# When GpSimd adds the squares of a new residual: after the input splits instead of among them

## The chip, the cores and the metric

The kernel runs on one core of one Trainium2 chip. The metric is the device time of one execution in microseconds (us), the median of several runs. A core has five engines that matter here: TensorE (PE in the profile; its weight loads are PEld), VectorE (DVE), ScalarE (ACT), GpSimd (POOL) and the DMA queue of SyncE (SP). They run side by side, each through its own list of instructions, and wait for each other on semaphores.

## The reference

Two stacks of two layers, one after the other, over 256 tokens (272 with 16 meta tokens in the first stack) with 1024 features, all in float32. In the second stack each branch ends in

```
h = h + weight * rms_norm(y, post_gain)       # y: output of an FFN, of the recurrent block or of attention
x = rms_norm(h, pre_gain)                     # input of the next branch
rms_norm(v, g) = v * rsqrt(mean(v * v) + 1e-6) * g
swiglu(x) = (silu(x @ w_gate) * (x @ w_up)) @ w_down
```

The branches of the second stack are, in order: FFN, recurrent block, FFN, keys and values with the next FFN, attention, FFN. Between two of them `h` gets a new value, and the next branch needs that value in two forms: as the input of its matrix products, and as the mean of its squares over the 1024 features.

## The kernel before, in words

The tensors lie transposed in SBUF: 128 features on the partitions, 8 slices of 128 features (k = 0 to 7), tokens along the free dimension. Each product of float32 tensors is made of three matmuls of split values: ScalarE rounds a tensor to its high part (`xhi`, `whi`), VectorE subtracts to get the low part (`xlo`, `wlo`), and TensorE adds up wlo x xhi, whi x xlo and whi x xhi. A tile of output (128 features) of an input of 8 slices is 24 matmuls. Weights stream through a ring of four slots: DMA to `raw`, ScalarE makes `whi` (line 885), VectorE makes `wlo` (line 1263).

The norm of the input is not put into the input. The matmuls run on `h` times its gain, and the factor 1/rms (`rstd`) is multiplied in when VectorE reads a tile out of PSUM. So the matmuls of a branch can begin before the sum of squares is there; the sum is only needed before the first tile is read.

The stages around the change are the six *updates*, numbered u = 7 to 12. Update 7 follows the first stack (VectorE scales `h` by the final norm, line 1768). Updates 8 to 12 add a branch output to `h` in VectorE's `update` (lines 1553 to 1587). For the slices 2 to 7 it works in pairs: scale a pair of `y` by `rstd` (line 1557), make the low parts of the pair before (line 1274), wait for its own pipeline, add into `h` (line 1562). After the low part of slice 7 it makes `wlo` of ring slot 3 of the next branch. These five updates have the same list of instructions. Meanwhile

- ScalarE (`inputs_from_h`, lines 1091 to 1104) makes the high parts of each pair (line 913) and then the squares of the pair (line 1104). The four pairs of squares go to `sil`, `z[0:2]`, `z[2:4]` and again `z[0:2]`; for the fourth it waits on `h_added` until GpSimd has read the second;
- GpSimd (`of_update`, lines 1807 to 1816) adds each pair of squares to `sil` as soon as ScalarE has made it (three adds of 128 x 512, line 1812), then adds the two halves of `sil` into `acc` (128 x 256, line 1816) and signals `sq_made`;
- TensorE runs `first_tiles` (lines 556 to 581): three tiles at once, 72 matmuls in the order of the slices, waiting before each slice for its low part (`x_lo_made`). Slices 6 and 7 come last, for tile 0, then 1, then 2. Then tile 3 (24 matmuls, lines 521 to 523), then `norm_sum` (line 532), which waits for `sq_made` and multiplies `acc` by a matrix of 1/1024. Behind it in TensorE's order stand tiles 4 to 7, which have PSUM banks of their own, and all later ones. `norm_sum` feeds ScalarE's square root (line 889), VectorE's reciprocal (line 1268), and by that the first reads of tiles.

ScalarE makes the next `whi` of slots 0, 1 and 2 when tiles 0, 1 and 2 are done; VectorE makes their `wlo` right after each; then comes the reciprocal, then slot 3. The order on every engine is the order of the program's lines; nothing is planned at run time.

In the listing, line numbers are those of the profile.

Of the kernel before, what the change touches and what calls it, by code (L numbers as in the profile page):

```python
# [19 lines left out]
T = SEQ + N_META  # L20
# [20 lines left out]
ALU = mybir.AluOpType  # L41
# [182 lines left out]
def program(nc, a):  # L224
    with ExitStack() as ctx:
# [4 lines left out]
        def at(name, shape, dt, where=None):  # L230

            place = top if where is None else where
            size = int(np.prod(shape[1:])) * (1 if dt == U8 else 4)
            h = nc.alloc_sbuf_tensor_at(name, shape, dt, offset=place[0])
            place[0] += (size + 31) // 32 * 32
            assert place[0] <= end, (name, place[0] - end)
            return h
# [11 lines left out]
        z = at("z", [P, 4, T], F32)  # L249
        sil = at("sil", [P, 2, T], F32)  # L250
        sqt = at("sqt", [P, 2, T], F32)
# [101 lines left out]
        def sem(name):  # L353
            return ctx.enter_context(nc.semaphore(name))
# [7 lines left out]
        h_made, x_hi_made, x_lo_made = sem("h_made"), sem("x_hi_made"), sem("x_lo_made")  # L362
        sq_made, sum_made, std_made, rstd_made = sem("sq_made"), sem("sum_made"), sem("std_made"), sem("rstd_made")

        y_sq, sq_added, h_sq, h_added = sem("y_sq"), sem("sq_added"), sem("h_sq"), sem("h_added")
        silu_made = sem("silu_made")
        hid_made, hid_hi_made, hid_lo_made = sem("hid_made"), sem("hid_hi_made"), sem("hid_lo_made")

# [40 lines left out]
        def layer_stage(l, which):  # L409
            q, j, n = ((0, 0, 0), (FFN_QUADS, FFN_TILES, 1), (FFN_QUADS + MIX_QUADS, FFN_TILES + MIX_TILES, 4))[which]  # L410
            return dict(q=l * LAYER_QUADS + q, j=l * LAYER_TILES + j, x=l * 3 + which, n=l * 5 + n,
                        f=l * 2 + which // 2, c=0)
# [466 lines left out]
        def _(act):  # L879
# [30 lines left out]
            def x_hi(x, k, c, to=xhi):  # L910

                at_k = bass.ds(k, 1) if not isinstance(k, int) else slice(k, k + 1)
                act.activation(to[:, at_k, c:T], h[:, at_k, c:T], ACT.Identity, scale=gain(x, k)).then_inc(x_hi_made, 1)  # L913
# [66 lines left out]
            def mixer(l):  # L980
                st = layer_stage(l, 1)
                q, j, x, n = st["q"], st["j"], st["x"], st["n"]
                for step, i in MIXER:
# [36 lines left out]
                    elif step == "turn_v":  # L1020
                        for s, (_, size) in enumerate(TOKEN_TILES):
                            act.wait_ge(v_turned, l * 3 + s + 1)
                            act.activation(vtok[0:size, s, :], bank[4 + s][0:size, :], ACT.Copy).then_inc(v_taken, 1)
# [23 lines left out]
                    elif step == "turn_v2":  # L1047
                        for s, (_, size) in enumerate(TOKEN_TILES):
                            act.wait_ge(v2_turned, l * 3 + s + 1)
                            act.activation(vtok2[0:size, s, :], bank[4 + s][0:size, :], ACT.Copy).then_inc(v2_taken, 1)  # L1050
# [40 lines left out]
            def inputs_from_h(x, u, c, to=xhi):  # L1091

                for s in range(4):
                    if s == 0:
                        act.wait_ge(h_made, 5 * (u - 7) + 1)
                        x_hi(x, 0, c, to)
                    act.wait_ge(h_made, 5 * (u - 7) + s + 2)
                    if s > 0:
                        x_hi(x, 2 * s, c, to)
                    x_hi(x, 2 * s + 1, c, to)  # L1100
                    if s == 3:
                        act.wait_ge(h_added, 3 * (u - 7) + 1)
                    squared = (sil[:, :, c:T], z[:, 0:2, c:T], z[:, 2:4, c:T], z[:, 0:2, c:T])[s]
                    act.activation(squared, h[:, 2 * s:2 * s + 2, c:T], ACT.Square).then_inc(h_sq, 1)

            def recurrent():
# [43 lines left out]
                for m in range(KD):  # L1150
# [3 lines left out]
                    if m == 7:  # L1154
                        norm_std(n + 1, c)
                    split_hi(q + 6 + m // RING, m % RING, CH8, j + 32 + m + 1)
                inputs_from_h(9, 9, c)

            def conv_hi(m):
# [21 lines left out]
            def attention():  # L1181
# [25 lines left out]
                for m in range(KD):  # L1207
                    act.wait_ge(tile_done, j + 8 + m + 1)
                    branch_out(n + 1, m, bank[4 + m % 2], j + 8 + m + 1, vcol("mix_post", 8 + m))
                    if m == 7:  # L1210
                        norm_std(n + 1, c)
                    split_hi(q + 3 + m // RING, m % RING, CH8, j + 8 + m + 1)
                inputs_from_h(13, 12, c)

            act.wait_ge(brow_done, 1)
# [18 lines left out]
            with act.Fori(0, DEPTH) as l:  # L1234
# [4 lines left out]
                ffn_down(**layer_stage(l, 2))  # L1239
            norm_std(10, 0)  # L1240
            inputs_from_h(7, 7, N_META)
            ffn(**F4)
            ffn_down(**F4, post=12)
# [551 lines left out]
        def _(pool):  # L1795
# [8 lines left out]
                        op = pool.tensor_tensor(acc[:, c:T], acc[:, c:T], sqt[:, k % 2, c:T], ALU.add)  # L1804
                op.then_inc(sq_made, 1)

            def of_update(u, last_sum):

                c = N_META
                for s in range(1, 4):  # L1810
                    pool.wait_ge(h_sq, 4 * (u - 7) + s + 1)
                    pool.tensor_tensor(sil[:, :, c:T], sil[:, :, c:T], z[:, 2 * ((s - 1) % 2):2 * ((s - 1) % 2) + 2, c:T],
                                       ALU.add).then_inc(h_added, 1)
                    pool.drain()
                pool.wait_ge(sum_made, last_sum)
                pool.tensor_tensor(acc[:, c:T], sil[:, 0, c:T], sil[:, 1, c:T], ALU.add).then_inc(sq_made, 1)

            def of_branch(n):

                c, done = N_META, branch_tiles(n) - 8  # L1820
                for m in range(1, 7):
                    pool.wait_ge(y_sq, done + m + 1)
                    pool.tensor_tensor(acc[:, c:T], acc[:, c:T], sqt[:, m % 2, c:T], ALU.add).then_inc(sq_added, 1)
                    if m < 6:
                        pool.drain()
                pool.drain().then_inc(sq_made, 1)

            def ffn(q, j, x, n, f, c, main_norm=True):
                with pool.Fori(0, KF // 2) as b:
                    for p in range(2):  # L1830
                        i = b * 2 + p
                        pool.wait_ge(silu_made, f * KF + i + 1)
                        pool.wait_ge(tile_read, b * RING + j + 2 * p + 2)
                        pool.tensor_tensor(z[:, 2 + p, c:T], sil[:, p, c:T], z[:, 2 + p, c:T],  # L1834
                                           ALU.mult).then_inc(hid_made, 1)
                        pool.wait_ge(hid_hi_made, f * KF + i + 1)
                        at_i = bass.ds(i, 1)
                        pool.tensor_tensor(hidlo[:, at_i, c:T], z[:, 2 + p:3 + p, c:T],  # L1838
                                           hidhi[:, at_i, c:T].bitcast(F32), ALU.subtract).then_inc(hid_lo_made, 1)
# [35 lines left out]
            def of_layer(st):  # L1875
                squares_of(h, 0, st["n"] + 1, lambda k: pool.wait_ge(tile_read, st["j"] + 2 * KF + k + 1))
# [9 lines left out]
            with pool.Fori(0, DEPTH) as l:  # L1886
# [2 lines left out]
                mixer(l)  # L1889
                ffn(**layer_stage(l, 2))  # L1890
                of_layer(layer_stage(l, 2))
            of_update(7, 11)
            ffn(**F4)
            of_branch(12)
            of_update(8, 13)
            for m in range(KD):
                pool.wait_ge(cv_hi_made, m + 1)
                pool.tensor_tensor(cvlo[:, m, :], cv[:, m, :], cvhi[:, m, :].bitcast(F32),
# [14 lines left out]
                    out_low(m - 1)  # L1913
            out_low(KD - 1)
            of_branch(14)
            of_update(9, 15)
            ffn(**F5)
            of_branch(16)
            of_update(10, 17)
            ffn(**F6)  # L1920
            of_branch(18)
            of_update(11, 19)
            of_branch(20)
            of_update(12, 21)
            ffn(**F7)
            of_branch(22)

# [81 lines left out]
```

## Time and profile before

| | |
|---|---|
| median of 3 runs | 2534.74 us (2528.47, 2534.74, 2535.23) |
| profiled execution | 2533.5 us, its span 2531.5 us |
| mean granted TensorE clock | 0.958 of full speed |
| TensorE busy | 93% of the span |
| VectorE, ScalarE, GpSimd busy | 59%, 47%, 24% |
| DMA | 150 GB/s over the span |

The span runs from the first instruction to the last of the profiled execution; every time of a row is counted from its start. An engine's busy time counts its instructions alone, not its waits. TensorE's clock has two levels, full (1.00 in the profile's column, 2.4 GHz) and half (0.50, 1.2 GHz). The end of a matmul is modelled, so for TensorE the distance from start to start is more telling than the time of one.

### The profile page before, as it was taken

The page shows a single profiled execution, that of the slowest core. Times are in us where ns is not written, and L with a number is a line of the kernel's source. Part 1 is how long each engine was busy: PE and PEld are TensorE (multiplying, and loading weights), DVE is VectorE, ACT ScalarE, POOL GpSimd, SP SyncE. Part 2 cuts the span into 40 slices and gives each one's busy share as a digit, 9 for nine tenths or more (in the row PEclk, how much of TensorE's full clock was granted, in tenths as well). Part 3 has the DMA queues.
Part 4 walks back from the last instruction along what each step waited for, and adds up shares of the span by engine and source line. Part 5 has one row for each costly group of instructions (what it writes and reads, how often), then busy time and mean ns, then how long its engine had stood idle before and what let it go on. Part 6 is the DMA issues. An engine that isn't in the chain of part 4 may idle for free.

```text
span 2531.5 us, 49922 instructions
## 1 busy us (share of the span) xinstructions
PE 2351.9 (93%) x18064; PEld 2266.5 (90%) x18064; DVE 1502.3 (59%) x1960; ACT 1191.4 (47%) x1739; POOL 604.3 (24%) x617
## 2 busy tenths in 40 slices
PE   7999988899999999879999989986899999977998
PEld 7999876699999999875899989986899899977998
DVE  6556775465555557873655565477654755465653
ACT  5445542344444436432354355456654545445552
POOL 4221130043213210310232233123331122111320
PEclk9999997899999999987999999998999999998999
DMA  6554332245545544321355445533455465531653
GB/s 209 174 183 156 115 116 66 67 160 182 178 158 174 191 145 147 100 92 42 109 178 182 164 148 190 193 118 116 151 192 198 147 202 184 197 117 63 200 195 108
DMA packets 99267, 380.27 MB, mean 150 GB/s; under 512 B 10911, under 2 KB 13087, under 8 KB 99144
## 3 DMA queue, kind: packets, MB, share of 16 engines
q1 hardware_dynamic: 99144, 378.63, 45.6%
q8 instruction: 77, 1.26, 0.2%
q14 instruction: 46, 0.38, 0.1%
HBM read 377.52 MB, written 3.16 MB: 150 GB/s over the span
## 4 chain that ended last, share of the span: by engine, by line
PE 63%; issue 25%; DVE 5%; POOL 4%; ACT 1%; POOLq 1%; DVEq 1%; DMA 0%; ACTq 0%; SPq 0%
PE bank L523 20%; PE bank L521 20%; PE bank L522 20%; POOL kd L1863 2%; DVE h L1562 1%; PE bank L564 1%; DVE xlo L1274 1%; PE bank L566 1%; PE bank L565 1%; POOL midlo L1871 1%; DVE rstd L1268 0%; DVE wlo L1263 0%; DVE y L1557 0%; POOLq L1802 0%; ACT whi L885 0%
## 5 line engine op out<-in xcount | busy, mean ns | idle before, releaser
L1263 DVE TENSOR_TENSOR wlo<-raw,whi 128x1024 fp32r<-128x1024 f32 (+1 forms) x660 | 886.5, 1353 | 525.3 <-ACT whi L885 523.6
L521 PE MATMUL bank<-xhi,wlo 128*128 128x272 f32 (+1 forms) x3392 | 981.6, 289 | 3.2 <-DVE wlo L1263 2.0
L523 PE MATMUL bank<-xhi,whi 128*128 128x272 f32 (+1 forms) x3392 | 976.3, 288 | 0.0
L522 PE MATMUL bank<-xlo,whi 128*128 128x272 f32 (+1 forms) x3392 | 974.3, 287 | 0.0
L885 ACT ACTIVATE whi<-raw 128x1024 fp32r<-128x1024 f32 (+1 forms) x660 | 728.8, 1117 | 452.9 <-PE bank L523 429.5
L521 PEld LDWEIGHTS bank<-xhi,wlo 128*128 128x128 f32 x3392 | 647.4, 191 | 5.0 <-DVE wlo L1263 2.3
L523 PEld LDWEIGHTS bank<-xhi,whi 128*128 128x128 f32 x3392 | 646.8, 191 | 0.0
L522 PEld LDWEIGHTS bank<-xlo,whi 128*128 128x128 f32 x3392 | 646.1, 190 | 0.4
L523 PE MATMUL bank<-hidhi,whi 128*128 128x272 f32 (+1 forms) x1408 | 400.1, 284 | 0.0
L521 PE MATMUL bank<-hidhi,wlo 128*128 128x272 f32 (+1 forms) x1408 | 399.9, 284 | 0.0
L522 PE MATMUL bank<-hidlo,whi 128*128 128x272 f32 (+1 forms) x1408 | 399.1, 283 | 0.0
L1834 POOL TENSOR_TENSOR z<-sil,z 128x272 f32<-128x272 f32 (+1 forms) x176 | 164.5, 935 | 600.9 <-DVE z L1300 471.8
L522 PEld LDWEIGHTS bank<-hidlo,whi 128*128 128x128 f32 x1408 | 265.5, 189 | 0.0
L523 PEld LDWEIGHTS bank<-hidhi,whi 128*128 128x128 f32 x1408 | 264.8, 188 | 0.0
L521 PEld LDWEIGHTS bank<-hidhi,wlo 128*128 128x128 f32 x1408 | 264.7, 188 | 0.0
L1838 POOL TENSOR_TENSOR hidlo<-z,hidhi 128x272 f32 (+1 forms) x176 | 167.1, 949 | 131.0 <-ACT hidhi L939 131.0
L913 ACT ACTIVATE xhi<-h,vec 128x256 fp32r<-128x256 f32 (+2 forms) x104 | 50.8, 512 | 245.0 <-DVE h L1318 176.4
L939 ACT ACTIVATE hidhi<-z 128x272 f32 (+3 forms) x176 | 74.8, 425 | 133.3 <-POOL z L1834 133.3
L1293 DVE TENSOR_TENSOR z<-bank,rstd 128x272 f32<-128x272 f32 (+1 forms) x176 | 75.8, 430 | 80.3 <-PE bank L523 79.9
L564 PE MATMUL bank<-xhi,wlo 128*128 128x256 f32 (+1 forms) x240 | 76.6, 319 | 42.3 <-DVE xlo L1274 30.5
L1300 DVE TENSOR_TENSOR z<-bank,rstd 128x272 f32<-128x272 f32 (+1 forms) x176 | 75.7, 430 | 63.2 <-PE bank L523 63.2
L1274 DVE SCALAR_TENSOR_TENSOR xlo<-h,vec,xhi 128x256 fp32r<-128x256 f32 (+2 forms) x104 | 63.9, 629 | 54.2 <-ACT xhi L913 54.2
(307 smaller groups left out, 2760.1 us busy)
## 6 DMA issues: line engine op xcount, KB each, us to landing
raw<-ffn_gu SPq DMA_DIRECT2D x352, 512.0 KB, 3.5
raw<-ffn_down SPq DMA_DIRECT2D x128, 704.0 KB, 4.1
raw<-mix SPq DMA_DIRECT2D x120, 512.0 KB, 3.5
raw<-rec SPq DMA_DIRECT2D x28, 512.0 KB, 4.0
raw<-kv SPq DMA_DIRECT2D x16, 512.0 KB, 4.2
raw<-att SPq DMA_DIRECT2D x16, 512.0 KB, 4.2
bias_rows<-rows SPq DMA_DIRECT2D x8, 256.0 KB, 4.3
bias<-bias_rows SPq DMA_DIRECT2D x1, 1536.0 KB, 7.9
```

What stands on the lines that cost most here:

```text
L521: pe.matmul(out, wlo[:, slot, w], xh(i), start=(i == 0), stop=False)
L522: pe.matmul(out, whi[:, slot, w], xl(i), start=False, stop=False)
L523: mm = pe.matmul(out, whi[:, slot, w], xh(i), start=False, stop=(i == last))
L564: pe.matmul(out, wlo[:, k, w], hi[:, i, at_c:], start=(i == 0), stop=False)
L885: act.activation(whi[:, k, 0:cols], raw[:, k, 0:cols], ACT.Copy).then_inc(hi_made, 1)
L939: act.activation(hidhi[:, at_i, c:T], z[:, 2 + p:3 + p, c:T], ACT.Copy).then_inc(hid_hi_made, 1)
L1263: dve.tensor_tensor(wlo[:, k, 0:cols], raw[:, k, 0:cols], whi[:, k, 0:cols].bitcast(F32), ALU.subtract).then_inc(lo_made, 1)
L1274: dve.scalar_tensor_tensor(to[:, at_k, c:T], h[:, at_k, c:T], gain(x, k), hi[:, at_k, c:T].bitcast(F32), ALU.mult, ALU.subtract).then_inc( ...
L1293: dve.tensor_tensor(z[:, p, c:T], bank[banks[2 * p]][:, 0:T - c], rstd[:, c:T], ALU.mult).then_inc(tile_read, 1)
L1300: dve.tensor_tensor(z[:, 2 + p, c:T], bank[banks[2 * p + 1]][:, 0:T - c], rstd[:, c:T], ALU.mult).then_inc(tile_read, 1)
L1834: pool.tensor_tensor(z[:, 2 + p, c:T], sil[:, p, c:T], z[:, 2 + p, c:T], ALU.mult).then_inc(hid_made, 1)
L1838: pool.tensor_tensor(hidlo[:, at_i, c:T], z[:, 2 + p:3 + p, c:T], hidhi[:, at_i, c:T].bitcast(F32), ALU.subtract).then_inc(hid_lo_made, 1)
```

## The change

GpSimd's `of_update` now waits, before its first add, until all eight low parts of the next input are made (`x_lo_made`, 8 for each input x), and then makes the same four adds in the same order. The fourth pair of squares goes to a buffer of its own, `sqt`, instead of `z[0:2]`, so that ScalarE need not wait for an add, and the semaphore `h_added` goes. The calls get the number of the input that the update makes: 7, 8, 9, 10, 12, 13.

```
# ScalarE, inputs_from_h
-                    if s == 3:
-                        act.wait_ge(h_added, 3 * (u - 7) + 1)
-                    squared = (sil[:, :, c:T], z[:, 0:2, c:T], z[:, 2:4, c:T], z[:, 0:2, c:T])[s]
+                    squared = (sil[:, :, c:T], z[:, 0:2, c:T], z[:, 2:4, c:T], sqt[:, :, c:T])[s]
                     act.activation(squared, h[:, 2 * s:2 * s + 2, c:T], ACT.Square).then_inc(h_sq, 1)
# GpSimd
-            def of_update(u, last_sum):
+            def of_update(u, x, last_sum):
                 c = N_META
-                for s in range(1, 4):
-                    pool.wait_ge(h_sq, 4 * (u - 7) + s + 1)
-                    pool.tensor_tensor(sil[:, :, c:T], sil[:, :, c:T], z[:, 2 * ((s - 1) % 2):2 * ((s - 1) % 2) + 2, c:T],
-                                       ALU.add).then_inc(h_added, 1)
+                pool.wait_ge(x_lo_made, 8 * x + 8)
+                for s, squared in enumerate((z[:, 0:2, c:T], z[:, 2:4, c:T], sqt[:, :, c:T])):
+                    pool.wait_ge(h_sq, 4 * (u - 7) + s + 2)
+                    pool.tensor_tensor(sil[:, :, c:T], sil[:, :, c:T], squared, ALU.add)
                     pool.drain()
                 pool.wait_ge(sum_made, last_sum)
                 pool.tensor_tensor(acc[:, c:T], sil[:, 0, c:T], sil[:, 1, c:T], ALU.add).then_inc(sq_made, 1)
# the calls
-            of_update(7, 11)
+            of_update(7, 7, 11)
...
-            of_update(12, 21)
+            of_update(12, 13, 21)
```

## Rows read from the trace of the kernel before

**Rows 1.** The page: busy time by engine, and the chain by engine.
```profile
PE 2351.9 (93%) x18064; PEld 2266.5 (90%) x18064; DVE 1502.3 (59%) x1960; ACT 1191.4 (47%) x1739; POOL 604.3 (24%) x617
...
PE 63%; issue 25%; DVE 5%; POOL 4%; ACT 1%; POOLq 1%; DVEq 1%; DMA 0%; ACTq 0%; SPq 0%
```

**Rows 2.** Timeline of VectorE in update 8: start, time, engine, line, operation, tiles, shapes.
```profile
1671.96 0.69 DVE L1562 SCALAR_TENSOR_TENSOR h<-y,h 128x512 f32<-128x512 f32 x1
...
1674.22 1.80 DVE L1562 SCALAR_TENSOR_TENSOR h<-y,h 128x512 f32<-128x512 f32 x1
...
1677.59 1.82 DVE L1562 SCALAR_TENSOR_TENSOR h<-y,h 128x512 f32<-128x512 f32 x1
1679.99 0.88 DVE L1274 SCALAR_TENSOR_TENSOR xlo<-h,vec,xhi 128x256 fp32r<-128x256 f32 x2 [0.58 <-ACT xhi L913]
1680.79 1.22 DVE L1263 TENSOR_TENSOR wlo<-raw,whi 128x1024 fp32r<-128x1024 f32 x1
```

**Rows 3.** Timeline of GpSimd in update 8; in brackets its idle time and releaser.
```profile
1674.19 1.28 POOL L1812 TENSOR_TENSOR sil<-sil,z 128x512 f32<-128x512 f32 x1 [15.59 <-ACT z L1104]
1677.57 1.29 POOL L1812 TENSOR_TENSOR sil<-sil,z 128x512 f32<-128x512 f32 x1 [2.09 <-ACT z L1104]
1680.95 2.22 POOL L1812 TENSOR_TENSOR sil<-sil,z 128x512 f32<-128x512 f32 x1 [2.09 <-ACT z L1104]
1683.33 1.52 POOL L1816 TENSOR_TENSOR acc<-sil 128x256 f32<-128x256 f32 x1 [0.16 <-issue]
1693.77 0.80 POOL L1898 TENSOR_TENSOR cvlo<-cv,cvhi 128x256 fp32r<-128x256 f32 x1 [8.92 <-ACT cvhi L1161]
```

**Rows 4.** Timeline of TensorE in update 8: start of tile 3, then the norm's sum.
```profile
1682.80 0.28 PE L521 MATMUL bank<-xhi,wlo 128*128 128x256 f32 x1
...
1685.63 0.59 PE L532 MATMUL bank<-acc,consts 128*128 128x256 f32 x2
```

**Rows 5.** Windows on TensorE, updates 7 to 12, first matmul to norm's sum: stretch, length, busy, clock.
```profile
1474.94:1488.79 13.85, 13.62 (x97) 0.85 0.04 7
1671.01:1685.63 14.62, 14.47 (x96) 0.79 0.13 40
1793.77:1808.41 14.64, 13.25 (x96) 0.90 0.14 40
1991.02:2005.64 14.62, 13.54 (x96) 0.88 0.13 40
2235.44:2250.07 14.63, 13.93 (x96) 0.83 0.13 41
2328.42:2343.03 14.61, 13.62 (x97) 0.86 0.14 41
```

**Rows 6.** Timeline of VectorE in short windows: first and second `wlo` after update 8.
```profile
1682.75 1.51 DVE L1263 TENSOR_TENSOR wlo<-raw,whi 128x1024 fp32r<-128x1024 f32 x1 [0.72 <-ACT whi L885]
...
1684.17 1.76 DVE L1263 TENSOR_TENSOR wlo<-raw,whi 128x1024 fp32r<-128x1024 f32 x1
```

**Rows 7.** Timeline of ScalarE after update 8: three `whi`.
```profile
1681.65 2.96 ACT L885 ACTIVATE whi<-raw 128x1024 fp32r<-128x1024 f32 x3 [0.78 <-PE bank L566]
```

**Rows 8.** Timelines of VectorE and GpSimd in update 7.
```profile
1476.96 0.48 DVE L1768 SCALAR_TENSOR_TENSOR h<-h,vec,rstd 128x256 f32<-128x256 f32 x1
...
1477.75 1.51 DVE L1768 SCALAR_TENSOR_TENSOR h<-h,vec,rstd 128x256 f32<-128x256 f32 x1
...
1485.55 0.74 POOL L1816 TENSOR_TENSOR acc<-sil 128x256 f32<-128x256 f32 x1 [0.16 <-issue]
```

**Rows 9.** Behind update 7: the `wlo` for tile 8 (VectorE), tile 8's first matmul (TensorE).
```profile
1498.24 1.23 DVE L1263 TENSOR_TENSOR wlo<-raw,whi 128x1024 fp32r<-128x1024 f32 x1 [3.58 <-ACT whi L885]
...
1500.54 0.28 PE L521 MATMUL bank<-xhi,wlo 128*128 128x256 f32 x1
```

**Rows 10.** A wait of TensorE (timeline), then the stretch behind it (windows, all engines).
```profile
1700.93 0.51 PE L521 MATMUL bank<-xhi,wlo 128*128 128x256 f32 x1 [1.97 <-DVE wlo L1263]
...
1701.00:1704.40 3.40, 3.40 (x16) 3.40 (x17) 3.25 (x7) 2.75 (x6) 1.47 (x2) 0.50 0.47 154
```

More of the change, by code:

```diff
@@ L363, in program @@
         sq_made, sum_made, std_made, rstd_made = sem("sq_made"), sem("sum_made"), sem("std_made"), sem("rstd_made")
-        y_sq, sq_added, h_sq, h_added = sem("y_sq"), sem("sq_added"), sem("h_sq"), sem("h_added")
+        y_sq, sq_added, h_sq = sem("y_sq"), sem("sq_added"), sem("h_sq")
         silu_made = sem("silu_made")
@@ L1891, in _ @@
                 of_layer(layer_stage(l, 2))
-            of_update(7, 11)
+            of_update(7, 7, 11)
             ffn(**F4)
             of_branch(12)
-            of_update(8, 13)
+            of_update(8, 8, 13)
             for m in range(KD):
@@ L1915, in _ @@
             of_branch(14)
-            of_update(9, 15)
+            of_update(9, 9, 15)
             ffn(**F5)
             of_branch(16)
-            of_update(10, 17)
+            of_update(10, 10, 17)
             ffn(**F6)
             of_branch(18)
-            of_update(11, 19)
+            of_update(11, 12, 19)
             of_branch(20)
-            of_update(12, 21)
+            of_update(12, 13, 21)
             ffn(**F7)
```

## The prediction, made before the changed kernel ran

> **What bounds the kernel now.** I read the page first. TensorE is busy 93% of the span and stands for 63% of the chain that ended last; GpSimd is 24% busy [rows 1]. So a change on GpSimd can pay or cost only where it moves TensorE. Then the timelines of all engines around the six updates, since the diff touches nothing else.
>
> Update 8 shows what the change is about. VectorE's add into h of a pair takes 0.69 us where GpSimd is idle, and 1.80 and 1.82 us where one of GpSimd's adds of squares began 0.02 to 0.03 us earlier [rows 2, 3]. GpSimd's add took 1.28 to 1.29 us, its usual time; VectorE was through 0.55 us after it. The later of the two waits for the whole of the earlier one. It goes the other way too: the third add began while VectorE made wlo, took 2.22 instead of 1.29 us, and ended 1.16 us after that wlo [rows 2, 3]. The page's 24% hides this: it is a collision in one place, twice in each update.
>
> TensorE feels it through the low parts of the slices 4 to 7. If none were late, the 96 matmuls from the start of the branch to the norm's sum would run on without a gap. Tile 3 gives the spacing at full clock: 24 matmuls in 2.83 us, 0.118 us each [rows 4]. Half clock doubles the array's share: 16 matmuls in 3.40 us, 0.213 us each [rows 10]. The time at half clock in each stretch is 2 x (1 - clock) x length: 4.2, 6.1, 2.9, 3.5, 5.0 and 4.1 us [rows 5]. A matmul at half clock loses 0.095 of its 0.213 us, so a stretch without waits takes 96 x 0.1185 = 11.4 us plus 0.44 of its half-clock time: 13.2, 14.1, 12.7, 12.9, 13.6 and 13.2 us. It took 13.85 and then about 14.6 us five times [rows 5]. The difference is what TensorE waits today: 0.6, 0.5, 2.0, 1.7, 1.0 and 1.4 us, 7.2 us in all. That is all the change can win there.
>
> **Part by part.** *ScalarE's wait on h_added goes, the fourth squares go to sqt.* Nothing either way: the second pair's add was over (1675.47) long before the fourth squares, and sqt has no other reader or writer until the next branch puts out y. No cost.
>
> *The first two adds leave VectorE's path.* Both adds into h should take 0.69 us again: 1.11 + 1.13 = 2.24 us, so the low part of slice 7, which ends at 1679.99 + 0.88 = 1680.87, ends at 1678.63 [rows 2]. The high parts follow h and move with it. In update 7 the same costs 1.51 - 0.48 = 1.03 us, twice: 2.06 us [rows 8].
>
> *All adds now begin after the last low part.* Call its end E: 1680.87 before, 2.24 us earlier after. Before, the sum was ready at 1683.33 + 1.52 = 1684.85, E + 3.98, and TensorE asked for it at 1685.63, E + 4.76 [rows 3, 4]: 0.78 us to spare. After, on the new E:
> - VectorE begins wlo of slot 3 before GpSimd sees the semaphore, as now, and ends at E + 1.14. The first add ends 1.16 us later, E + 2.30, just as the third one did [rows 2, 3].
> - Second add from E + 2.46 (0.16 us between two of GpSimd's instructions, rows 3) to E + 3.75.
> - The next wlo (slot 0) follows tile 0. Before, it began at 1682.75, E + 1.88 [rows 6]. Tile 0 now comes earlier by TensorE's lost waits, while E comes 2.24 us earlier, so it is asked for at E + 4.1 less 0.5 to 2.0, E + 2.2 to E + 3.6. It then waits for the second add and ends about 1.09 us later, as 1682.75 + 1.51 did behind the add that ended 1683.17 [rows 3, 6]: E + 4.84.
> - Third add, asked for at E + 3.91, waits for it: E + 6.00. The wlo of slot 1 goes next, since it was waiting: E + 7.09. ScalarE's three whi, 0.98 us apart, are ready in time [rows 7]. That the two engines take turns is seen now: the final add, alone 0.74 us, took 1.52, ending 0.59 us behind the first wlo, and the second wlo then took 1.76 us [rows 3, 6, 8].
> - Final add: E + 7.68, TensorE's sum at about E + 7.73.
>
> On the old E that is E + 5.49: 0.73 us later than now. It costs 0.73 us in each of updates 8 to 12, 3.65 us. The order is close in one place: where tile 0 is earliest (update 9, wlo asked for at E + 2.2, before the second add at E + 2.46), wlo goes first, one more wlo stands before the end, and the sum comes 0.8 us later still. I take that once: 0.8 us. In update 7 there is no wlo of slot 3. The adds run in a row to about E + 4.3, the final one waits for one wlo, E + 5.95; TensorE arrives at E + 4.77 + 2.06 - 0.6 = E + 6.2. No wait, 0.6 us won. What hides the rest there is the wlo of tile 8, ready at 1499.47 for a matmul at 1500.54 [rows 9]; that 1.07 us shrinks by 0.6 and by about 0.2 us of a later reciprocal, and still holds. Without that cover the 0.6 us is worth nothing.
>
> Bounds for the price of the five: below, GpSimd never blocked, with the last add at E + 0.1 + 3 x 1.45 + 0.74 = E + 5.2, about TensorE's earliest arrival, so TensorE keeps the 6.6 us; above, wlo first every time, 1.53 us each, 7.65 us. I take 0.73, nearest to what rows 3 and 6 show of turns.
>
> Behind the waiting instruction: on TensorE tiles 4 to 7, ready to run, so the wait is a real loss. On GpSimd the next work idled 8.92 us before it [rows 3]; nobody notices. ScalarE's root and VectorE's reciprocal move by 0.6 to 0.7 us with the sum. SP's queue waits on wlo only, and these move by under a microsecond against a ring of four.
>
> *The clock.* This wait is longer than the shift, since TensorE now arrives earlier: 0.73 plus its lost waits, 1.2, 2.7 (3.5 if wlo goes first), 2.4, 1.8 and 2.1 us in updates 8 to 12. Now there is none in this place. A wait of 1.97 us elsewhere was followed by 3.40 us at 0.50, in which 16 matmuls ran where 28.7 fit: 1.5 us lost [rows 10]. Three of the five waits are as long; whether one lowers the clock depends on where it falls. I take one or two: 1.5 x 1.5 = 2.3 us. Bounds: 0, and four times 1.5 = 6 us.
>
> The Trainium skill (TensorE: Matmul & The Clock Gate, "Why this matters for your kernels") asks only that idle gaps between bursts stay under some 3 us. By that rule no wait here but the 3.5 us one would cost clock, and the sum would lose its 2.3 us. The row with 1.97 us speaks against it.
>
> **Sum.** 3.65 + 0.8 - 0.6 + 2.3 = 6.15 us on 2533.5 us of the profiled execution (span 2531.5): 2539.7. The median of the runs shown, 2534.74, is 1.2 us above that execution: 2541.
>
> **The rivals.**
> - *The adds fit* (other side: faster). GpSimd isn't held up by the wlo, TensorE finds its sum at E + 5.2, and all lost waits come back: -7.2 us, 2527.5. For: GpSimd's adds alone need only 5.1 us. Against: four wlo fall into the same 8 us, and now a single one costs an add 0.93 us [rows 3]. It decides where GpSimd gets two of its adds in unblocked after the slot 0 wlo is asked for.
> - *The clock stays up throughout.* +3.9 us, 2538.6. This is the skill's rule above as a mechanism. Against it stands the 1.97 us row.
> - *The clock falls in three or more of the waits* (clearly slower). 3.85 + 3 to 4 x 1.5 = +8.4 to +10, and with wlo first in another update or two up to +12: 2543 to 2547. For: waits of 2.1 to 2.7 us where 1.97 was enough. Against: update 8's 1.2 and update 11's 1.8 us are shorter, and a TensorE wait of 1.2 us cannot be one of them if 1.97 is near the edge. From the third fall on, the change is slower than can be mistaken.
> - *It doesn't do what it says*: VectorE's add into h stays at 1.8 us for another reason, so E doesn't move and the adds end at E + 7.7, some 3 us late each: +15 us, 2550. The 0.69 us row and the matching ends speak against it.
>
> **How the numbers follow.** Forecast 0.45; clock stays up 0.15; three or more falls 0.25; adds fit 0.10; not what it says 0.05. A measurement of this kernel tells about 0.3% (7.6 us) from no change. Faster by more: half of "the adds fit" and a little, 0.06. Slower by more: 0.25 + 0.05 + 0.01 = 0.31. Within: 0.63. The range holds the forecast, the clock cases and a part of the gain: 2530 to 2548; the runs shown already spread over 7 us.
>
> **What would show it.** Right: line 1562 at 0.69 us for every pair; low part of slice 7 some 2.2 us sooner after its update's start; GpSimd's first and third adds over 2 us, the final one about 1.5; line 532 with idle time before it, released by GpSimd, in updates 8 to 12 and not in 7; stretches from first matmul to sum of about 15.4 us instead of 14.6, and 13.2 in update 7. Wrong: no idle before line 532, or stretches under 14 us.

## The result, and the profile after

The changed kernel takes 2539.14 us in the median of 20 runs (2532.55 to 2544.81), the kernel before 2535.20 us (20 runs, 2528.47 to 2539.78). The ratio is 1.0018 with a 95% interval of 1.0010 to 1.0025: slower by some 4 us, inside the 0.3% that the prediction called no change, and clear of zero.

The six stretches from a branch's first matmul to its norm's sum, on TensorE, in the changed kernel (stretch, length, busy time and matmuls, granted clock, DMA share, GB/s); they answer to [rows 5]:

```profile
1476.34:1489.66 13.32, 13.32 (x97) 0.84 0.01 2
1671.88:1688.18 16.30, 13.05 (x97) 0.90 0.28 94
1796.17:1811.46 15.29, 13.92 (x97) 0.83 0.20 65
1994.17:2009.45 15.28, 13.91 (x96) 0.83 0.21 66
2239.37:2254.67 15.30, 14.20 (x97) 0.81 0.21 66
2333.04:2348.33 15.29, 13.47 (x96) 0.86 0.21 66
sum 90.78, PE 81.87; mean PE 13.65
```

Update 7 is 0.5 us shorter than before, update 8 is 1.7 us longer, the other four are 0.65 us longer each. The sum is 90.78 us against 86.97: +3.8 us, as much as the timed difference of 3.9. Between them nothing grew: from each norm's sum to the next branch's first matmul, and from the last sum to the end of the span, each part is within 0.2 us of its length before, +0.3 us in all six. The busy time tells what fills the stretches: in update 7 TensorE is busy throughout, in the others 1.1 to 3.25 us are missing. The timeline names who is waited for, in updates 8 and 9; the third row is the first matmul of tile 4 behind the sum:

```profile
1688.17 0.70 PE L532 MATMUL bank<-acc,consts 128*128 128x256 f32 x2 [3.25 <-POOL acc L1814]
...
1811.46 0.70 PE L532 MATMUL bank<-acc,consts 128*128 128x256 f32 x2 [1.37 <-POOL acc L1814]
1811.81 0.47 PE L521 MATMUL bank<-xhi,wlo 128*128 128x256 f32 x1
```

Before, TensorE came to that matmul 0.78 us after the sum was ready [rows 3, 4]. VectorE in update 9 of the changed kernel, and below it the next two `wlo` in short windows:

```profile
1799.37 0.69 DVE L1560 SCALAR_TENSOR_TENSOR h<-y,h 128x512 f32<-128x512 f32 x1
...
1801.63 0.69 DVE L1560 SCALAR_TENSOR_TENSOR h<-y,h 128x512 f32<-128x512 f32 x1
1802.90 0.88 DVE L1272 SCALAR_TENSOR_TENSOR xlo<-h,vec,xhi 128x256 fp32r<-128x256 f32 x2 [0.58 <-ACT xhi L913]
1803.70 1.22 DVE L1261 TENSOR_TENSOR wlo<-raw,whi 128x1024 fp32r<-128x1024 f32 x1
...
1807.05 1.54 DVE L1261 TENSOR_TENSOR wlo<-raw,whi 128x1024 fp32r<-128x1024 f32 x1 [2.13 <-ACT whi L885]
1808.51 2.31 DVE L1261 TENSOR_TENSOR wlo<-raw,whi 128x1024 fp32r<-128x1024 f32 x1
```

The last two rows are the `wlo` of slots 0 and 1. GpSimd in the same update, one row for each of its four adds:

```profile
1803.86 2.21 POOL L1811 TENSOR_TENSOR sil<-sil,z 128x512 f32<-128x512 f32 x1 [15.19 <-ACT sqt L1102]
...
1806.21 1.29 POOL L1811 TENSOR_TENSOR sil<-sil,z 128x512 f32<-128x512 f32 x1
...
1807.64 2.09 POOL L1811 TENSOR_TENSOR sil<-sil,sqt 128x512 f32<-128x512 f32 x1
1809.88 1.52 POOL L1814 TENSOR_TENSOR acc<-sil 128x256 f32<-128x256 f32 x1
```

The add into `h` takes 0.69 us each time (1.80 and 1.82 in [rows 2]), and the last low part ends 7.61 us after the branch's first matmul, where it was 9.86 in update 8 [rows 2, 5]. So the change does what it says. What it gains there is spent behind: the last low part ends at 1803.78, the final add at 1811.40, 7.62 us later; before it was 3.98. Of the four adds three are blocked behind a `wlo`, and the `wlo` of slots 0 and 1 each behind an add. Only the second add went free.

Updates 10 to 12 go the same way. In update 8 the `wlo` of slot 0 comes 0.07 us ahead of the second add, and the add waits for it (VectorE, then GpSimd):

```profile
1681.87 1.23 DVE L1261 TENSOR_TENSOR wlo<-raw,whi 128x1024 fp32r<-128x1024 f32 x1 [1.23 <-ACT whi L885]
...
1681.94 2.31 POOL L1811 TENSOR_TENSOR sil<-sil,z 128x512 f32<-128x512 f32 x1
```

So all four adds are blocked there, and the stretch is 1.0 us longer than the other ones.

### The profile page after: what moved, and what is told of

Read it like the earlier page. It is cut to its first block, busy times and chain, and to the rows that moved or that the text cites. A ratio compares the mean times of both kernels' runs of the same rounds, so it can differ in the third digit from the quotient of the medians.

```text
span 2537.0 us, 49928 instructions
## 1 busy us (share of the span) xinstructions
PE 2355.1 (93%) x18064; PEld 2268.9 (89%) x18064; DVE 1496.7 (59%) x1960; ACT 1190.8 (47%) x1739; POOL 609.4 (24%) x617
## 4 chain that ended last, share of the span: by engine, by line
PE 61%; issue 26%; POOL 4%; DVE 3%; POOLq 2%; ACT 2%; DVEq 1%; DMA 0%; ACTq 0%; SPq 0%
PE bank L523 20%; PE bank L521 20%; PE bank L522 19%; POOL kd L1861 2%; POOLq L1812 1%; POOL midlo L1869 1%; PE bank L564 1%; PE bank L565 1%; PE bank L566 1%; DVE rstd L1266 1%; POOLq L1800 0%; DVE h L1560 0%; DVE cv L1594 0%; ACT whi L885 0%; DVE wlo L1261 0%
```

## The experiments

Theory T (turns): the price of the change is the order in which GpSimd's adds and VectorE's `wlo` follow each other behind the last low part, whole instruction by whole instruction. Rival C (clock): it is mostly half clock behind TensorE's new waits. In all of them, "stretches" means the sum of the six stretches above; it is 86.97 us before and 90.78 in the changed kernel. One profiled execution can't show 4 us by its span; the stretches can.

**The changed kernel once more.** No edit.

> The changed kernel once more. Theory T (turns): the sum of squares is late by turns between GpSimd's adds and VectorE's wlo; TensorE's sum starts 7.7 us after the last low part (8.7 where wlo of slot 0 comes before the second add), in updates 8 to 12, whatever the clock does; +4 us, 1.0016 of the kernel before. How often a wait before the sum is followed by half clock changes from execution to execution: 0 to 2 of the five. Rival C (clock): the extra time is mostly half clock behind the waits; then a profile with none of these falls would be within 1 us of the kernel before.

2538.97 us (11 runs) against 2535.38, ratio 1.0017 (1.0008 to 1.0026). Stretches 91.04 us:

```profile
1470.54:1484.02 13.48, 13.48 (x97) 0.83 0.01 3
1666.24:1682.60 16.36, 13.12 (x97) 0.90 0.27 92
1790.62:1805.91 15.29, 13.99 (x96) 0.82 0.19 67
...
sum 91.04, PE 83.04; mean PE 13.84
```

The stretches repeat to 0.2 us in each update. In update 12 they do so at a granted clock of 0.80 here and 0.86 in the first profile, since the end of the stretch is set by GpSimd and no longer by TensorE. This also answers rival C: behind four of the five waits TensorE ran on at full clock in both profiles, and only the wait of 3.24 us in update 8 was followed by half clock, as in the first profile. No profile was without that one fall, so the case that rival C named did not occur; it falls because the extra time stands inside the stretches, ahead of the sum. The span of this execution was 2529.9 us, 7 us under that of the first profile and below the 2531.5 of the kernel before, though the program is slower: 5.8 us of the difference stand before update 7 begins (1476.34 against 1470.54), while the six stretches together are 0.3 us longer than in the first profile.

**The buffer alone.** The kernel before, with this on ScalarE and the adds reading `z[0:2]`, `z[2:4]`, `sqt` as soon as each is made:

```
-                    if s == 3:
-                        act.wait_ge(h_added, 3 * (u - 7) + 1)
-                    squared = (sil[...], z[:, 0:2, c:T], z[:, 2:4, c:T], z[:, 0:2, c:T])[s]
+                    squared = (sil[...], z[:, 0:2, c:T], z[:, 2:4, c:T], sqt[:, :, c:T])[s]
```

> Of the two parts only the buffer: fourth squares to sqt, no wait on h_added, adds still as soon as each pair of squares is made. Theory T: no change, within 2 us (ratio 1.000), line of the add into h still 1.8 us for two pairs, sum asked for 4.76 us after the last low part. Rival: if sqt or the missing wait were what costs, this kernel would show the 4 us.

2536.64 us (12 runs), ratio 1.0004 (0.9994 to 1.0013). Stretches 86.96 us, the same as before to 0.01; each one is within 0.02 us of its own in [rows 5]. The adds into `h` of two pairs still take 1.82 us in update 8. The buffer costs and gives nothing that these runs can tell. What costs is when the adds begin.

**No adds.** The changed kernel without the three adds of pairs; the final add of the two halves of `sil` stays, so the sum of squares holds only the first pair.

```
                 pool.wait_ge(x_lo_made, 8 * x + 8)
-                for s, squared in enumerate((z[:, 0:2, c:T], z[:, 2:4, c:T], sqt[:, :, c:T])):
-                    pool.wait_ge(h_sq, 4 * (u - 7) + s + 2)
-                    pool.tensor_tensor(sil[:, :, c:T], sil[:, :, c:T], squared, ALU.add)
-                    pool.drain()
+                pool.wait_ge(h_sq, 4 * (u - 7) + 4)
```

> Leaves out GpSimd's three adds of the pairs of squares, so the sum holds the first pair of squares only; the last add (halves of sil) still waits for the last low part. Measures the ceiling. Theory T: VectorE's adds into h take 0.69 us, the last low part comes 2.24 us (2.06 in update 7) sooner, no wait before the sum; all of TensorE's lost waits come back, 7.2 us less than before: 2528, ratio 0.997. Rival R1 (the low parts are not the limit, the add into h is slow for another reason): within 2 us of before. Rival C: like T but less, since more half clock falls on the matmuls: -4 to -7 us.

2525.42 us (5 runs), ratio 0.9958 (0.9945 to 0.9970).

```profile
1675.09:1687.91 12.82, 12.82 (x96) 0.88 0.16 47
1795.83:1809.60 13.77, 13.77 (x97) 0.81 0.14 45
...
sum 78.75, PE 78.74; mean PE 13.12
```

TensorE is busy through every stretch, and the stretches are 8.2 us shorter than before (7.2 had been worked out from the old execution's clock). The median fell by 10.0 us; 8.2 lies inside the interval of the ratio. This is the ceiling: the low parts of slices 4 to 7 do hold TensorE up, and they are late through GpSimd.

**The halves on TensorE.** The changed kernel without the final add; TensorE sums both halves of `sil`.

```
+                    pe.matmul(bank[NORM][:, 0:T - c], mean, sil[:, 0, c:T], start=True, stop=False)
+                    pe.matmul(bank[NORM][:, 0:T - c], mean, sil[:, 1, c:T], start=False, stop=True).then_inc(sum_made, 1)
...
-                pool.tensor_tensor(acc[:, c:T], sil[:, 0, c:T], sil[:, 1, c:T], ALU.add).then_inc(sq_made, 1)
```

> The changed kernel without GpSimd's last add: TensorE sums the two halves of sil by two matmuls into the same bank. Theory T: the third add ends 6.0 us after the last low part instead of 7.7 for the last one; TensorE asks at 5.0 to 6.5, so it waits 0 to 1 us. Per update 1.4 us less than in the changed kernel less 0.25 us for the second matmul, in five updates -5.9 us, in update 7 +0.25: 2533.5, i.e. about 2 us under the kernel before, ratio 0.999. Rival C: the same order of waits, so falls of the clock would stay; then no better than the changed kernel by more than 3 us.

2534.07 us (12 runs), ratio 0.9995 (0.9985 to 1.0005): 4.9 us less than the changed kernel, against 5.65 expected. It fits, though in a less simple way than expected:

```profile
1672.99:1687.41 14.42, 12.82 (x96) 0.90 0.22 74
1795.89:1810.29 14.40, 12.82 (x96) 0.90 0.24 75
1993.44:2008.00 14.56, 12.97 (x96) 0.89 0.21 78
2238.37:2252.00 13.63, 13.38 (x97) 0.85 0.13 41
...
sum 83.94, PE 78.45; mean PE 13.08
```

The stretches are 6.8 us shorter than in the changed kernel, but two lengths stand side by side. Where the clock is at 0.89 to 0.90 of full (updates 8 to 10), tile 0 is done early, the `wlo` that follows it comes before the second add, and one turn more stands before the sum: 14.4 to 14.6 us. Where it is 0.85 and 0.87 (updates 11 and 12) that `wlo` comes after: 13.6. A faster TensorE makes its own sum later. And the second matmul costs more than the 0.25 us assumed. Here is the sum on TensorE in update 9:

```profile
1810.29 0.70 PE L592 MATMUL bank<-sil,consts 128*128 128x256 f32 x2 [1.58 <-POOL sil L1819]
1810.83 0.59 PE L593 MATMUL bank<-sil,consts 128*128 128x256 f32 x2
1811.07 0.47 PE L521 MATMUL bank<-xhi,wlo 128*128 128x256 f32 x1
```

From the first to tile 4 it is 0.78 us. The single matmul of the changed kernel, also after a wait, took 0.35 (1811.46 to 1811.81), so the second one costs 0.43 us. The parts between the stretches are 0.3 to 0.6 us longer each than before the change, 3.2 us in all (six times 0.43 is 2.6 of them), and that takes back the 3.0 us that the stretches are shorter than before: hence the time of the kernel before. Waits of 1.6 us stood in three updates here, and none was followed by half clock.

**One add early.** The changed kernel, but the first add goes at once:

```
-                pool.wait_ge(x_lo_made, 8 * x + 8)
...
+                    if s == 1:
+                        pool.wait_ge(x_lo_made, 8 * x + 8)
```

> The changed kernel, but GpSimd's first add goes at once, as before; the second, third and last wait for the last low part. Theory T: one of VectorE's two adds into h takes 1.8 us, the other 0.69, so the last low part comes 1.1 us sooner than before. After it two adds and the last one take turns with the wlo: sum about 5.5 us after it, 0.4 us sooner than before the change in updates 8 to 12, and 0.5 in update 7: 2.5 us under the kernel before, 2533, ratio 0.999. Rival C (clock behind waits): there is no wait left, so it says the same; it is not told apart here. Rival: the number of adds behind the last low part doesn't matter, only that one is held back: then +4 us as in the changed kernel.

2538.74 us (12 runs), ratio 1.0015 (1.0002 to 1.0028): the 2.5 us gain wasn't there. VectorE, and then GpSimd, in update 9:

```profile
1798.57 1.82 DVE L1560 SCALAR_TENSOR_TENSOR h<-y,h 128x512 f32<-128x512 f32 x1
...
1801.95 0.69 DVE L1560 SCALAR_TENSOR_TENSOR h<-y,h 128x512 f32<-128x512 f32 x1
...
1805.97 1.52 DVE L1261 TENSOR_TENSOR wlo<-raw,whi 128x1024 fp32r<-128x1024 f32 x1 [0.73 <-ACT whi L885]
```

```profile
1804.25 2.16 POOL L1812 TENSOR_TENSOR sil<-sil,z 128x512 f32<-128x512 f32 x1 [4.41 <-ACT sqt L1102]
1806.55 2.09 POOL L1812 TENSOR_TENSOR sil<-sil,sqt 128x512 f32<-128x512 f32 x1
1808.79 1.52 POOL L1815 TENSOR_TENSOR acc<-sil 128x256 f32<-128x256 f32 x1
```

With one collision left, TensorE waits for a low part once more (0.25 us in update 9; 1.39 us in all before the change), and `wlo` of slot 0 is asked for 1.86 us after the last low part (1805.97), as before the change and ahead of the second of the late adds (1806.55). So all three late adds are blocked and the sum starts 6.26 us after the last low part, not 5.5. Stretches 88.28 us, 1.3 more than before. That is inside the interval of the ratio, whose middle lies higher, at about 4 us. This profile has another 2.1 us between the sum of update 11 and the first matmul of update 12: 80.43 us at a mean clock of 0.84, against 78.35 at 0.90 before. Whether that comes from the edit isn't shown, since the two profiles of the changed kernel differ there by 1.6 us as well. The expectation had put `wlo` behind the add; the turns were right, their order wrong.

**The sum later in TensorE's order.** The changed kernel, with the sum after tile 4 in all branches of the second stack:

```
-                    if t == 3:
+                    if t == 4:
                         input_norm(x, n, c)()
...
-                    if c and t == 3 and main_norm:
+                    if c and t == 4 and main_norm:
```

> The changed kernel, but TensorE makes the sum after tile 4 instead of after tile 3 (in all branches of the second stack), so that it doesn't wait for GpSimd. Theory T: the wait before the sum goes, but the sum itself comes 1.0 to 2.3 us later after the start of the branch than in the kernel before; all of the slack of the wlo for tile 8 (1.1 us) is used up, so TensorE waits there instead: 0 to +4 us against the kernel before, 2535 to 2539. Rival (only the wait in TensorE's order costs): all of the 7 to 8 us of lost waits come back, 2527.

2538.92 us (12 runs), ratio 1.0020 (1.0012 to 1.0029). TensorE in update 9 and at tile 8 behind it:

```profile
1813.05 0.70 PE L532 MATMUL bank<-acc,consts 128*128 128x256 f32 x2 [0.46 <-POOL acc L1814]
...
1823.93 0.38 PE L521 MATMUL bank<-xhi,wlo 128*128 128x256 f32 x1 [1.67 <-DVE wlo L1261]
```

The wait before the sum is 0.46 us instead of 1.37, and a new one of 1.67 us stands before tile 8. The `wlo` it needs hangs on the sum by the reciprocal, the first reads and ScalarE's work behind them, and the sum now comes 16.35 us after the first matmul instead of 15.29. The time is that of the changed kernel, and the rival's 2527 is out: the sum's own time is what counts, not only its place in TensorE's list.

**The adds on VectorE.** The four adds move to VectorE, behind its `wlo` of slot 3; GpSimd does nothing in an update.

```
+            def of_update(u, last_sum):                      # VectorE
+                c = N_META
+                for s, squared in enumerate((z[:, 0:2, c:T], z[:, 2:4, c:T], sqt[:, :, c:T])):
+                    dve.wait_ge(h_sq, 4 * (u - 7) + s + 2)
+                    dve.tensor_tensor(sil[:, :, c:T], sil[:, :, c:T], squared, ALU.add)
+                    dve.drain()
+                dve.wait_ge(sum_made, last_sum)
+                dve.tensor_tensor(acc[:, c:T], sil[:, 0, c:T], sil[:, 1, c:T], ALU.add).then_inc(sq_made, 1)
...
             update(12, F4["j"] + FFN_TILES, 0.5, 8, next_q=REC["q"])
+            of_update(8, 13)
```

> The four adds of the squares on VectorE, after the wlo of slot 3 (in update 7 after the last low part); GpSimd does nothing in an update. Theory T: no two engines want the port, adds into h 0.69 us; four adds of 0.6, 0.6, 0.6 and 0.35 us with their drains are ready 3.7 us after the last low part, TensorE asks at 5.2 to 6.5, so no wait and no held-up wlo that TensorE needs: as without adds, -8 to -10 us, 2526, ratio 0.996. Rival (VectorE is the bound behind an update): the wlo of slots 0 to 2 and the reciprocal are 1 to 2 us late and TensorE waits at tile 4 or 8: within 2 us of the kernel before.

2527.37 us (11 runs) against 2534.38, ratio 0.9967 (0.9957 to 0.9977): 7 us less than before, where 8 to 10 were expected. It beats both kernels. VectorE in update 9:

```profile
1803.72 1.22 DVE L1261 TENSOR_TENSOR wlo<-raw,whi 128x1024 fp32r<-128x1024 f32 x1
1804.86 1.45 DVE L1592 TENSOR_TENSOR sil<-sil,z 128x512 f32<-128x512 f32 x2
1806.38 0.69 DVE L1592 TENSOR_TENSOR sil<-sil,sqt 128x512 f32<-128x512 f32 x1
1807.15 0.42 DVE L1595 TENSOR_TENSOR acc<-sil 128x256 f32<-128x256 f32 x1
1807.49 3.49 DVE L1261 TENSOR_TENSOR wlo<-raw,whi 128x1024 fp32r<-128x1024 f32 x3
```

And its stretches on TensorE:

```profile
1796.19:1809.64 13.45, 13.45 (x96) 0.83 0.12 40
...
sum 78.36, PE 78.35; mean PE 13.06
```

VectorE makes the four adds in 2.7 us, where GpSimd took 7.5 in the changed kernel; three `wlo` in a row take 3.49 us, where they took 5.44 in the changed kernel; the sum is ready at 1807.57, 2 us before TensorE asks. The stretches are as short as with no adds at all, 78.36 us against 78.75.

## Why the prediction was right, and where not

The time was forecast at 2541 and is 2539.1, and the direction and the mechanism were the forecast ones. The forecast difference was 6.15 us and the measured one 3.9; the part that was too much is the clock's. By its steps:

- *The first two adds leave VectorE's path, 2.24 us.* Right: 0.69 us for every pair, last low part 7.61 us after the first matmul against 9.86.
- *TensorE's waits today, 7.2 us.* Right in kind, a little low: 8.2 us came back without adds. The half-clock time that the formula takes in is the execution's own: fed with the clocks of the kernel without adds, it gives that kernel's stretches to 0.1 us each.
- *Sum of squares at E + 7.7.* Right to the tenth: the four adds began at E + 0.08, 2.43, 3.86 and 6.10 in update 9 (forecast 0.1, 2.46, 3.91, then 6.16), and the sum started at E + 7.7 in updates 9 to 12. The turns could be read from one add, one final add and two `wlo` of the kernel before [rows 3, 6].
- *0.73 us in each of five updates, one extra turn of 0.8 us.* Measured 0.65 to 0.68 us in four and 1.7 us in one. The extra turn came in update 8, not 9: this time it was update 8 that had the least half clock (0.90), so its tile 0 was early. Which update it hits follows the clock of the execution: both profiles of the changed kernel had it in update 8, at 0.90, and with the halves on TensorE it stood in the three updates at 0.89 to 0.90.
- *Update 7: 0.6 us won, covered.* 0.53 and 0.37 us; no wait before the sum, and from the sum to update 8's first matmul it is 182.22 us, as before, so the gain was kept.
- *The clock, 2.3 us.* This is the term that was mis-sized: its measure is about zero. Only the 3.25 us wait of update 8 was followed by half clock. Windows of the changed kernel behind updates 8, 12 and 9, all engines:

```profile
1689.00:1692.40 3.40, 3.40 (x19) 3.40 (x18) 2.89 (x2) 1.33 (x2) 0.00 (x0) 0.53 0.36 136
2348.90:2352.30 3.40, 3.40 (x31) 3.40 (x30) 3.09 (x3) 2.71 (x3) 0.00 (x0) 1.00 0.72 240
1812.20:1815.60 3.40, 3.40 (x31) 3.40 (x30) 3.09 (x3) 2.70 (x3) 0.00 (x0) 1.00 0.76 260
```

After the waits of 1.81 and 1.37 us TensorE ran on at full clock. And the one fall cost nothing: from update 8's sum to the next branch's end it is 101.9 us, as before (102.1), both at a mean clock of 0.88. In the recurrent block TensorE waits for VectorE and its `wlo` soon after [rows 10], and it gave the loss back there: the 1.18 us wait 10.25 us behind the sum is gone, and the one of 1.97 is shorter. That shorter wait was not followed by half clock either, so the branch has one fall less there and one more behind the sum. Below it the same place without adds, where a wait as long as in [rows 10] was not followed by half clock:

```profile
1703.36 0.39 PE L521 MATMUL bank<-xhi,wlo 128*128 128x256 f32 x1 [1.62 <-DVE wlo L1261]
1703.40:1706.80 3.40, 3.35 (x26) 3.14 (x27) 3.25 (x7) 2.76 (x5) 1.47 (x2) 1.00 0.43 159
...
1703.01 0.38 PE L521 MATMUL bank<-xhi,wlo 128*128 128x256 f32 x1 [2.02 <-DVE wlo L1261]
1703.10:1706.50 3.40, 3.34 (x27) 3.14 (x28) 3.25 (x7) 2.75 (x6) 1.47 (x2) 1.00 0.44 154
```

The kernel without adds had neither fall, and from its sum to the first matmul of update 9 it took 107.9 us; the changed kernel took 108.0 with a fall and the kernel before 108.1 with one. So a fall behind this sum cost 0.2 us at most, not 1.5. Two steps of the clock term failed. The waits were taken from the old execution's clock: 2.7 and 2.4 us in updates 9 and 10 where 1.4 were met, since these stretches now held 5.2 us of half clock instead of 2.9 and 3.5. And the price of a fall was counted in full for whichever wait it followed, also where the stage behind has slack. Without the term the forecast would have been +3.85 us; the stretches say +3.8. A slip in the recorded working: 0.73 plus 1.0 is 1.7 for update 11, not 1.8.

On the rule that idle gaps under some 3 us are harmless (the Trainium skill, TensorE: Matmul & The Clock Gate, "Why this matters for your kernels"): before the sums the runs went its way, with only the waits of 3.25 and 3.24 us followed by half clock. The 1.97 us wait of [rows 10] stands against it as a rule for all cases. Waits of 2.0 us in that same place were followed by half clock in four profiles (before, buffer alone, halves on TensorE, one add early) and not in two (no adds, adds on VectorE), so in these runs the length of a wait alone does not decide. The prediction also applied the rule wrongly: its sum held one wait of 3.5 us, so by that rule it would have kept one fall, 1.5 us, of its 2.3.

The rival "the adds fit" fell with GpSimd's rows, since only one of its four adds went unblocked; "not what it says" with the 0.69 us; "three or more falls" with the windows; "the clock stays up" came nearest, at +3.9 us, though the clock fell once: its number is right because that fall cost nothing.

## What to carry to other kernels

When two engines block each other, moving one's work behind a critical stretch moves the collision too: list what the other engine has to do in the new place, lay both out in turns, and see when the last one ends and who asks for it. Before moving, ask whether the blocked engine could do the work itself: 2.7 us on VectorE replaced 7.5 us on GpSimd, blocked time included, and the stretches became as short as without any adds. Changes of a few us are read from stretches between fixed instructions, not from one execution's span; the six here repeat to 0.2 us. See first that a stretch repeats: the one from update 11's sum to update 12's first matmul was 78.4 and 76.7 us in two profiles of the same kernel, at a mean clock of 0.90 and 0.93.

## What the runs showed that was not expected

The same program spanned 2537.0 us in one profiled execution and 2529.9 in another, at 0.957 and 0.962 of the clock, with stretches equal to 0.3 us in sum. And an engine that runs faster can be served later: at 0.85 of the clock the sum came 13.6 us after the first matmul, at 0.90 14.4 us, since the earlier `wlo` got in ahead of an add.
